# Expert routing of a two-layer decoder trunk: table lookups on 16-bit whole numbers, and the gate-spreading loops written out on every engine with comparison scalars read in place

## The reference

```
q = einsum('td,dn->tn', x, wq).reshape(T, 8, 2, 128)
s1 = einsum('thd,hkd->thk', q[:, :, 0], keys[0]);  s2 = the same with q[:, :, 1], keys[1]
v1, i1 = top_k(s1, 16);  v2, i2 = top_k(s2, 16)
cand = (v1[..., :, None] + v2[..., None, :]).reshape(T, 8, 256)
cidx = (i1[..., :, None] * 128 + i2[..., None, :]).reshape(T, 8, 256)
top_s, pos = top_k(cand, 16)
eidx = take_along_axis(cidx, pos);  gate = softmax(top_s)
y[t] = sum over (h, k) of gate * gelu(u_tab[eidx] . x[t]) * v_tab[eidx]
```

## Time and profile before

| | us |
|---|---|
| median of 3 runs (lowest, highest) | 4130.28 (4129.97, 4134.26) |
| the profiled execution | 4124.39 |
| its span | 4122.7 |
| PE, DVE, ACT, POOL busy in the span | 3860.1, 2796.9, 1486.5, 1341.2 |
| routing, layer 0 (first ACT operation to the next stage's) | 826.0 to 1054.7 |
| spreading, layer 0 | 1054.7 to 1215.8 |
| routing and spreading, layer 1 | 2875.3 to 3102.7, 3102.7 to 3263.8 |
| mean granted TensorE clock | 0.972 of full |

### The profile page before, as it was taken

The page is one execution under the profiler, slowest core; times in us unless marked ns, Lnnn a source line. Parts: engine busy times, 40 slices in busy tenths (PEclk is TensorE's granted clock), DMA queues, the critical chain, the costliest instruction groups (busy, mean ns, idle before and its releaser), DMA issues. The chain is left out here.

```text
span 4122.7 us, 55217 instructions
## 1 busy us (share of the span) xinstructions
PE 3860.1 (94%) x19618; PEld 3374.7 (82%) x19618; DVE 2796.9 (68%) x5400; ACT 1486.5 (36%) x2152; POOL 1341.2 (33%) x1148
## 2 busy tenths in 40 slices
PE   8989899999789999999899898999997899999996
PEld 7867687899788999988778666878997889999885
DVE  3255435399988888877642654352999788888776
ACT  2233322244663333333322334222436633333332
POOL 1010000066675555533100200000657555555321
PEclk9999999999999999999999999999999999999998
DMA  3210322254469999999622203232544799999994
GB/s 143 82 61 26 128 92 100 102 179 159 147 233 361 358 354 339 344 333 336 231 104 82 69 19 135 92 114 91 184 167 152 256 358 355 350 346 338 333 333 171
DMA packets 266694, 840.58 MB, mean 204 GB/s; under 512 B 20000, under 2 KB 69152, under 8 KB 241440
## 3 DMA queue, kind: packets, MB, share of 16 engines
q1 hardware_dynamic: 192800, 570.02, 38.8%
q0 software_dynamic: 73728, 268.47, 17.6%
HBM read 751.90 MB, written 86.51 MB: 203 GB/s over the span
## 5 line engine op out<-in xcount | busy, mean ns | idle before, releaser
L88 PE MATMUL bank<-v_high,w_high 128*128 128x512 f32 x1536 | 598.1, 389 | 0.0
L87 PE MATMUL bank<-v_low,w_high 128*128 128x512 f32 x1536 | 598.1, 389 | 0.0
L1046 POOL TENSOR_TENSOR ahead_u_low<-merged,ahead_u_high 128x1024 fp32r<-128x1024 f32 x96 | 256.7, 2690 | 1047.9 <-ACT ahead_u_high L1041 1047.9
L89 PE MATMUL bank<-v_high,w_low 128*128 128x512 f32 x1536 | 597.4, 389 | 0.0
L1091 POOL DMA_INDIRECT far_rows<-peer_v_dram,far_index x256 | 372.2, 1454 | 501.8 <-DVE x_far L1115 457.1
L1091 POOL DMA_INDIRECT far_rows<-peer_u_rows_dram,far_index x256 | 369.2, 1442 | 344.0 <-DVE far_dots L1097 292.2
L1733 DVE TENSOR_TENSOR v_low<-v_raw,v_high 128x1024 fp32r<-128x1024 f32 x256 | 301.8, 1221 | 241.0 <-ACT v_high L1672 241.0
L1672 ACT ACTIVATE v_high<-v_raw 128x1024 fp32r<-128x1024 f32 x256 | 257.1, 1052 | 508.0 <-PE bank L89 508.0
L87 PE MATMUL bank<-xT_low,u_high 128*128 128x384 f32 x1088 | 371.9, 342 | 19.1 <-ACT hid L1660 10.0
L89 PE MATMUL bank<-xT_high,u_low 128*128 128x384 f32 x1088 | 371.0, 341 | 0.0
L88 PE MATMUL bank<-xT_high,u_high 128*128 128x384 f32 x1088 | 370.6, 341 | 0.0
(11 more groups left out here) (358 smaller groups left out, 8481.7 us busy)
## 6 DMA issues: line engine op xcount, KB each, us to landing
merged<-peer_u_dram SPq DMA_DIRECT2D x128, 1024.0 KB, 5.3
v_raw<-peer_v_dram SPq DMA_DIRECT2D x128, 1024.0 KB
gates_scratch<-stage SPq DMA_DIRECT2D x12, 4096.0 KB, 14.4
G<-gates_scratch SPq DMA_DIRECT2D x64, 768.0 KB
in_raw<-w_in_dram SPq DMA_DIRECT2D x40, 1024.0 KB, 5.2
mg_raw<-w_merge_dram SPq DMA_DIRECT2D x44, 768.0 KB, 4.2
hidden_scratch<-ahead_hid SPq DMA_DIRECT2D x60, 384.0 KB, 2.4
hid<-hidden_scratch SPq DMA_DIRECT2D x30, 768.0 KB, 6.9
```

The costliest lines, as they stand in the source:

```text
L87: nc.tensor.matmul(out, lh, rl, start=first, stop=False)
L88: nc.tensor.matmul(out, lh, rh, start=False, stop=False)
L89: return nc.tensor.matmul(out, ll, rh, start=False, stop=last)
L1046: eng.tensor_tensor(self.ul[:, c], self.ur[:, c], as_f32(self.uh[:, c]), ALU.subtract).then_inc(self.u_low, 1)
```

## The change

In routing, the places and the lists become 16-bit whole numbers (`place`, `lists`, U16), laid out with the 16 list entries outermost, so that the comparison is with a constant table `entry` (16x128, made once by POOL with an `iota` behind the fifth `low`). The reduction over 16 becomes four additions of halves, the last one into fp32. The candidates get a buffer of their own, and `gate` and the pairs are ordered (k, h) in place of (h, k). In spreading, all loops are written out on all engines, the copies of scalars with their waits and POOL's drain are gone, and each comparison takes its scalar straight from `rowT`, `colT`, `gateT`.

```
-                    V.tensor_copy(best_ixf[:], best_ix[:])
+                    V.tensor_copy(lists[:].rearrange("p two k h -> p h two k"), best_ix[:].rearrange("p (h two) k -> p h two k", two=2))
...
+                    V.tensor_copy(place[:, 0, :].rearrange("p (k h) -> p h k", h=H), rankf[:, 0, :].rearrange("p (h k) -> p h k", h=H))
+                    link(V.tensor_tensor(place[:, 1, :].rearrange("p (k h) -> p h k", h=H), rankf[:, 1, :].rearrange("p (h k) -> p h k", h=H),
+                                         rankf[:, 3, :].rearrange("p (h k) -> p h k", h=H), ALU.add))
+                    if t == 0:
+                        dve.wait_ge(entries, 1)
                     for side, dst in enumerate((row, col)):
-                        link(V.tensor_tensor(hit, rankf[:, side, :].unsqueeze(2).to_broadcast([P, H * K, K]),
-                                             iota_row[:, 0:K].unsqueeze(1).to_broadcast([P, H * K, K]), ALU.is_equal))
-                        link(V.tensor_tensor(hit.rearrange("p (h k) j -> p h k j", h=H),
-                                             hit.rearrange("p (h k) j -> p h k j", h=H),
-                                             lists[:, :, side, :].unsqueeze(2).to_broadcast([P, H, K, K]), ALU.mult))
-                        link(V.tensor_reduce(dst[:], hit, AX, ALU.add))
+                        link(V.tensor_tensor(hit[:], place[:, side:side + 1, :].to_broadcast([P, K, PAIRS]), entry[:], ALU.is_equal))
+                        link(V.tensor_tensor(hit[:].rearrange("p j (k h) -> p j k h", h=H), hit[:].rearrange("p j (k h) -> p j k h", h=H),
+                                             lists[:, side].unsqueeze(2).to_broadcast([P, K, K, H]), ALU.mult))
+                        for half in (8, 4, 2):
+                            link(V.tensor_tensor(hit[:, 0:half], hit[:, 0:half], hit[:, half:2 * half], ALU.add))
+                        link(V.tensor_tensor(dst[:], hit[:, 0], hit[:, 1], ALU.add))
...
-            with eng.Fori(0, NTB // 2 - 1) as m:
-                pair(m, False)
-            pair(NTB // 2 - 1, True)
+            for m in range(NTB // 2):
+                pair(m, m == NTB // 2 - 1)
+
+        def scalar_of(v, n, s):
+
+            return v[:, n * STEP + s:n * STEP + s + 1]
...
-                        nc.gpsimd.tensor_copy(rows[:, g % 2, :], rowT[:, ds(n * STEP + 4 * g, 4)])
-                        pool.drain()
-                        for s in range(4):
-                            ins = nc.gpsimd.tensor_scalar(hot_row[:, 4 * g + s, :], iota_row[:], rows[:, g % 2, s:s + 1], None, ALU.is_equal)
+                        for s in range(4 * g, 4 * g + 4):
+                            ins = nc.gpsimd.tensor_scalar(hot_row[:, s, :], iota_row[:], scalar_of(rowT, n, s), None, ALU.is_equal)
...
-                    dve.wait_ge(cols_hot, 4 * n + 4)
-                    nc.vector.tensor_copy(cols[:, 0, :], colT[:, ds(n * STEP, STEP)])
-                    nc.vector.tensor_copy(cols[:, 2, :], rowT[:, ds(n * STEP, STEP)])
-                    nc.vector.tensor_copy(cols[:, 1, :], gateT[:, ds(n * STEP, STEP)]).then_inc(chain, 1)
-                    dve.wait_ge(chain, n + 1)
...
-                            ins = nc.vector.tensor_scalar(hot_col[:, s, :], iota_row[:], cols[:, 0, s:s + 1], cols[:, 1, s:s + 1],
+                            ins = nc.vector.tensor_scalar(hot_col[:, s, :], iota_row[:], scalar_of(colT, n, s), scalar_of(gateT, n, s),
                                                           ALU.is_equal, ALU.mult)
...
-                    nc.scalar.activation(row_of[:], rowT[:, ds(n * STEP + 4, 4)], ACT.Copy).then_inc(chain_a, 1)
-                    act.wait_ge(chain_a, 2 * n + 1)
-                        ins = nc.scalar.activation(distance[:, s, :], iota_row[:], ACT.Abs, scale=-1.0, bias=row_of[:, s:s + 1])
+                        ins = nc.scalar.activation(distance[:, s, :], iota_row[:], ACT.Abs, scale=-1.0, bias=scalar_of(rowT, n, 4 + s))
```

More of the change, by code:

```diff
@@ L1129, in route_stage @@
         best_ix = sb(ctx, "best_ix", [P, N_LISTS, K], U32)
-        best_ixf = sb(ctx, "best_ixf", [P, N_LISTS, K])
-        hits = sb(ctx, "hits", [P, H, K * K])
+        lists = sb(ctx, "lists", [P, 2, K, H], U16)
+        cand = sb(ctx, "cand", [P, H, N_CAND])
+        hit = sb(ctx, "hit", [P, K, PAIRS], U16)
+        entry = sb(ctx, "entry", [P, K, PAIRS], U16)
         top = sb(ctx, "top", [P, H, K])
@@ L1135, in route_stage @@
         rankf = sb(ctx, "rankf", [P, 4, H * K])
-        cand = hits[:, :, 0:N_CAND]
-        hit = hits[:].rearrange("p h (k j) -> p (h k) j", j=K)
+        place = sb(ctx, "place", [P, 2, PAIRS], U16)
         row = sb(ctx, "row", [P, PAIRS])
         col = sb(ctx, "col", [P, PAIRS])
-        gate = sb(ctx, "pgate", [P, H, K])
+        gate = sb(ctx, "pgate", [P, K, H])
         total = sb(ctx, "total", [P, H])
         keys_in = sem("rt_keys_in")
+        entries = sem("rt_entries")
         scored = sem("rt_scored")
@@ L1177, in _ @@
                     ahead.low(pool, chunk // EC, chunk % EC)
+                    if chunk == EC:
+                        nc.gpsimd.iota(entry[:], pattern=[[1, K], [0, PAIRS]], base=0, channel_multiplier=0).then_inc(entries, 1)
                     if chunk == PER_TILE + 2:
@@ L1198, in turn @@
                     for j, src in enumerate((row, col, gate)):
-                        v = src[:] if j < 2 else src[:].rearrange("p h k -> p (h k)")
+                        v = src[:] if j < 2 else src[:].rearrange("p k h -> p (k h)")
                         nc.tensor.transpose(bank[3][:, j * P:(j + 1) * P], v, ident[:]).then_inc(turned, 1)
@@ L1334, in _ @@
                     dve.wait_ge(expd, t + 1)
-                    link(V.tensor_reduce(total[:], gate[:], AX, ALU.add))
+                    link(V.tensor_reduce(total[:], gate[:].rearrange("p k h -> p h k"), AX, ALU.add))
                     link(V.reciprocal(total[:], total[:]))
-                    weights = gate[:] if t else far.gate[:].rearrange("p (h k) -> p h k", h=H)
-                    link(V.tensor_tensor(weights, gate[:], total[:].unsqueeze(2).to_broadcast([P, H, K]), ALU.mult))
+                    weights = gate[:] if t else far.gate[:].rearrange("p (k h) -> p k h", h=H)
+                    link(V.tensor_tensor(weights, gate[:], total[:].unsqueeze(1).to_broadcast([P, K, H]), ALU.mult))
                     if t:
@@ L1353, in spread_stage @@
         hot_col = sb(ctx, "hot_col", [P, STEP, P])
-        cols = sb(ctx, "cols", [P, 3, STEP])
-        rows = sb(ctx, "rows", [P, 2, 4])
-        row_of = sb(ctx, "row_of", [P, 4])
         distance = sb(ctx, "distance", [P, 4, P])
@@ L1365, in spread_stage @@
         stored = [sem(f"sp_stored{b}") for b in range(2)]
-        chain = sem("sp_chain")
         TURNS = TB // STEP
@@ L1390, in body @@
                         pool.wait_ge(spread, 4 * n + g + 1)
-                        nc.gpsimd.tensor_copy(rows[:, g % 2, :], rowT[:, ds(n * STEP + 4 * g, 4)])
-                        pool.drain()
-                        for s in range(4):
-                            ins = nc.gpsimd.tensor_scalar(hot_row[:, 4 * g + s, :], iota_row[:], rows[:, g % 2, s:s + 1], None, ALU.is_equal)
+                        for s in range(4 * g, 4 * g + 4):
+                            ins = nc.gpsimd.tensor_scalar(hot_row[:, s, :], iota_row[:], scalar_of(rowT, n, s), None, ALU.is_equal)
                         ins.then_inc(rows_hot, 1)
-                with pool.Fori(0, NTB * TURNS) as n:
+                for n in range(NTB * TURNS):
                     body(n)
@@ L1496, in _ @@
                     sp.sem_inc(ahead.h_out[r], 16)
-                with sp.Fori(0, NTB // 2 - 1) as m:
-                    pair(m, False)
-                pair(NTB // 2 - 1, True)
+                for m in range(NTB // 2):
+                    pair(m, m == NTB // 2 - 1)
     return [(stored[b], 16 * (NTB // 2) + 16) for b in range(2)], [(ahead.h_out[b], 16 * AHEAD_SPREAD + 16) for b in range(2)]
```

10 lines of the change are left out of this document (5 added, 5 removed).

## The result

| | us | ratio to before, 95% interval |
|---|---|---|
| before, median of 4 runs (lowest, highest) | 4130.12 (4128.98, 4134.26) | |
| changed, median of 4 runs | 4089.61 (4085.93, 4093.87) | 0.990 (0.9883 to 0.9918) |
| changed, profiled execution; its span | 4085.93; 4084.1 | |

A forecast was written before the change was run, and what follows sets the result against it. DVE was taken to bound routing, and DVE, POOL and PE at nearly one pace spreading, DVE slightly slowest. Gains of 2 x (9.0 + 11.6) = 41 us off 4130.3 gave 4089 us, range 4077 to 4110.

The forecast's parts named there:

- Spreading: Spreading stage: without copies and waits PE becomes the bound at 5.69 us a turn; gain 11.6 us a layer.
- The stall that I let remain: Spreading, ten turns with a `low`: POOL needs 6.1 us against PE's 5.69; 0.45 each, 4.5 in all.
- that cost stays: Start of spreading: PE's idle shrinks from 19 to 10 us, its clock falls to half all the same; no gain.
- POOL starved: Rival, spreading: without DVE's pauses POOL's comparisons wait and become the bound; 26 us a layer lost, 4164 us; chance 0.03.
- Routing: Routing stage: DVE's saving ends its last wait until SP's store bounds the stage; gain 9.0 us a layer.
- DVE can't use what it saves in tiles 0 and 1: Routing: only tiles 2 and 3 count; their two lookups must fall from 34.1 to 26.3 us.
- the wait that was named: Routing: tile 2's L1310 on DVE waits for PE's transposes of tile 1, at 3023.4; it ran at 3025.01.
- Tile 3: Routing, last lookup on DVE: no `low` is left, 16-bit operations at double pace; 8.5 us, was 13.9.
- Tile 2: Routing, lookup on DVE beside POOL's `low`: 15 us taken, between 8.5 and 16; was 20.2.
- the ceiling: Routing's end: SP's last store limits the gain to 9.3 us in layer 0, 8.8 in layer 1.
- fp32 pace: Rival, routing: 16-bit operations run at fp32 pace, lookup saves nothing; +6 to -7 us a layer, 4107 us; chance 0.10.
- The three rivals that were faster than before but less so: 16-bit at fp32 pace, 4107 us (0.10); spreading gains only 4.7 a layer, 4103 (0.08); routing only 4, 4099 (0.07).

The follow-up runs named there:

- spreading only: The routing stage of before with the changed spreading; 4106.16 us, ratio to before 0.9943.
- all copies back: The changed kernel with every copy, drain and wait of the old spreading put back into the written-out turns; 4110.05 us.
- lookup only: The changed routing with the spreading stage of before; 4115.71 us, ratio to before 0.9966.
- reduction: The changed kernel with one 16-bit tensor_reduce in place of the four halving additions of each side; 4095.34 us.
- start and reduction: The changed kernel with DVE's first groups and ACT's rows ahead of their weight parts in spreading, plus one 16-bit tensor_reduce a side in routing; 4092.87 us.
- PE kept at work: The changed kernel with 48 more matmuls that nothing reads, in PE's waits at routing's end and spreading's start; 4087.54 us.
- POOL only writes: The changed kernel with POOL's `low` in routing replaced by a fill with zeros, that part of the weights left out; 4084.92 us.

## Why the prediction was right, and where not

- **Spreading: right in mechanism, mis-sized by 2.5 us.** Of 14.07 us, 12.76 came between the third groups of turns 0 and 23 (forecast 11.0), 0.95 from turn 0 (forecast 0, as "that cost stays"), 0.36 from the start (forecast 0.6). The stall that I let remain, 0.45 in each of ten turns, measured 0.33 (turns of 6.02 against 5.69), and 2.7 in the stage where 4.5 were taken. It is POOL's, as forecast: in such a turn PE starts group 3 0.10 us after POOL's last comparison, when `hot_col` had been ready for 2.5 us. But PE alone is not the bound. The forecast's own figures for DVE, 5.27 and 6.35, make 11.62 for two turns against PE's 11.38; two turns measured 11.71, and DVE idles 1.1 us in the stage. That DVE's copies and waits were the bound, not the loops, is shown: DVE's copies alone restore the old time.
- **Turn 0: luck, as far as the runs show.** It ran 7.47 us instead of 8.42 because the full clock was granted 3.58 us after its first matmul instead of 5.66. That PE had idled less is not the reason: in "spreading only", with the old idle time, the two layers took 8.58 and 7.22, and in "all copies back", with the new one, 8.64 and 7.64. No run here shows what sets that moment, so nothing shows that the 0.95 (1.00 in layer 1) is owed to the change, and it would not come again for sure.
- **POOL starved (3%): it did not happen**; a comparison takes 0.598 us. But "the trace agrees with it only for the two-input `low`" is wrong. In routing, operations of DVE with one input are held off too when POOL's `low` has started first: before the change the cast of the key numbers (L1287) took 0.30 us at least and 2.42 at most, and in the changed kernel a `tensor_scalar` that takes 0.19 took 2.42 once, until 0.1 us after the end of the `low`. There the trace agrees with the Trainium skill (SBUF — State Buffer, section on who interferes with whom), which has casts and `tensor_scalar` in a two-port mode and a GpSimd operation shut each other out. In spreading the comparisons show nothing of it (POOL's take 0.598 us beside DVE's and 0.60 with DVE idle, DVE's 0.40 at most), and why is open. Operations with one input, changed kernel (duration ns least/median/most):

```profile
L1319 DVE TENSOR_SCALAR rank<-pos x8: 185/194/2419, 862.8 to 3062.6; 128x128 uint32<-128x128 uint32 x8
L1328 DVE CAST place<-rankf x8: 455/1502/2670, 864.6 to 3064.4; 128x128 uint16<-128x128 f32 x8
```

- **Routing: the amount right, the account wrong in part.** L1310 was not waiting for PE's transposes: it came 1.6 us after their end, and no wait is listed for it. In the changed kernel L1315 comes 1.7 us after them, 149.87 us into the stage in place of 150.45 (layer 1: 149.75, 149.73), where the forecast had it 1.6 sooner. But the transposes are a floor close below. Where DVE came sooner it waited for them, and its shift began 148.2 to 148.3 us into the stage each time: in layer 1 of "lookup only", in one layer each of "reduction", "start and reduction" and "PE kept at work", and in both where POOL only writes. Waits of DVE in routing, "lookup only", layer 1:

```profile
DVE pgate L1315 <- PE bank L1205: 1.6, 1, 1.6
```

- **What the tiles gave.** The lookups save 2.9, 1.1, 3.2 and 5.2 = 12.4 us in layer 0; what stands ahead of them grew by 1.1 a tile where I took 0.3 (0.61 between L1315 and the first comparison, with the two operations on `place` at 1.02 us together; 0.37 in the cast of the lists and the addition behind it; 0.13 in L1315, which writes in the new order), 4.4 in all. The remaining 8.0 is near the 8.84 measured. Of the 4.0 us of tiles 0 and 1 nothing is left by tile 2: its lookup begins 154.83 us into the stage before and after the change (layer 1: 154.09 and 154.82), as the longer operations and other meetings with `low` have used it up. So "DVE can't use what it saves in tiles 0 and 1" came true, though not by the wait that was named. DVE ended its part 8.6 us sooner, where the forecast's terms give 11.6.
- **Tile 3 right, tile 2 mis-sized.** 8.68 against 8.5. Tile 2 took 17.1, not 15, so DVE, not SP's store, ended routing, and PE waited 3.0 us where I had put under 1. That the ceiling lay only 1.1 us further (the run where POOL writes) is why the sum still held.
- **fp32 pace: the rival was far too mild.** It had "+6 to -7 a layer" and 4107; the same operations in fp32 give -28.7 a layer and 4160. Tiles 2 and 3 took 46.5 us where at most 42 were taken, and tile 2's lookup began 19 us later: the rival counted two tiles of four, and a loss in tiles 0 and 1 has no floor to hide behind. The three rivals that were faster than before but less so are all excluded by their marks: 1.22 us, spreading under 150 in the changed kernel, routing over 7.6.
- **Scatter of routing.** Twelve stages ran the changed routing as it is: ten took 219.7 to 220.1 us, two 222.7 and 222.8. In one of these (layer 1 of "lookup only") tile 2's L1315 comes 1.6 us sooner than in the changed kernel and tile 3's lookup 2.5 later: the chain meets POOL's `low` at other places, at some 2.1 us each, and to be early gains nothing.

## What to carry to other kernels

A wait that the trace doesn't list can still stand just below: compare the start of an operation with the end of everything it needs, and the difference is how much of a saving can be used. A loss has no such limit, so give a slower rival the account of all tiles. When three engines run at one pace, take each one's edit back alone; here the smallest-looking pieces, three copies of 0.2 us, carried the whole stage because their engine had no pause. A faster DVE operation with two SBUF inputs is worth its full saving only where POOL isn't reading: the lookup that takes 8.7 us alone took 17.1 beside it.

## What the hardware showed that I had not expected

- A POOL operation that reads SBUF holds off a DVE operation with two SBUF inputs, one that only writes does not: 17.1 us against 8.68 for the same lookup. This is what the Trainium skill (SBUF — State Buffer, section on who interferes with whom) says, and the trace agrees. A fill is also shorter (0.95 us against 2.4), so a part could be its length; but not one of the 96 operations of the eight lookups was lengthened. Operations with one input were, in that same run: two `tensor_scalar` that take 0.22 and 0.19 us took 0.52 and 0.45, until a fill had ended.
- Two operations that write 128 16-bit values each at a stride of 8 elements take 1.02 us together (the second shows 0.88), where an addition of 128 fp32 values side by side shows 0.29.
- A reduction over 16 values that lie 256 bytes apart takes 3.6 to 3.7 us for 2048 16-bit elements; the fp32 one over neighbours took 2.29. No run separates the type from the distance.
- The 16-bit `tensor_tensor` of 2048 elements took 1.22 us, with a broadcast operand and in pieces of 8 as well; this is what the Trainium skill (VectorE: DVE Perf Modes, section on the perf-mode tier table) gives, 1224 ns.
